# Output projection of a hybrid encoder layer: nine of twelve tile transposes as 32x32 blocks on DVE and quadrant copies on POOL

## The reference

```python
x = x + jnp.concatenate([a, p], axis=-1) @ w_out      # a: attention, p: pooling mixer
h2 = rmsnorm(x, norm2_g)
x = x + jnp.square(jax.nn.relu(h2 @ w_up)) @ w_down   # w_up: 1024 x 4096
```

## Time and profile before

| | |
|---|---|
| median of 3 runs | 1484.53 us (1484.3 to 1484.99) |
| the profiled execution | 1483.54 us, of which the trace spans 1481.8 us |
| PE busy in the span | 1471.5 us (99%) |
| DVE, ACT, POOL busy | 1042.6, 705.7, 401.1 us |
| granted TensorE clock | 1.00 |

### The profile page before, as it was taken

How to read it: one execution, slowest core, us unless ns; L and a number is a source line. 1 busy time by engine, 2 the same in 40 slices (tenths; PEclk the granted TensorE clock), 3 DMA queues, 4 the chain that set the end, 5 groups by cost and what they waited for, 6 DMA issues and landing times.

```text
span 1481.8 us, 23179 instructions
## 1 busy us (share of the span) xinstructions
PE 1471.5 (99%) x7884; PEld 1312.3 (89%) x7884; DVE 1042.6 (70%) x1301; ACT 705.7 (48%) x1195; POOL 401.1 (27%) x347
## 2 busy tenths in 40 slices
PE   9999999999999999999999999999999999999999
PEld 8999878888888889999999999999888888888887
DVE  6766799999856675544454545448888878878875
ACT  6223399999833344545454545456322322323220
POOL 3467599888910010000000000001320311311300
PEclk9999999999999999999999999999999999999999
DMA  8654331000246639343334323347744343343434
GB/s 262 154 121 112 98 90 24 20 11 14 83 146 250 219 113 413 132 146 125 129 113 157 134 109 134 137 155 291 264 157 153 104 149 122 125 156 105 137 99 183
DMA packets 89066, 209.10 MB, mean 141 GB/s; under 512 B 8240, under 2 KB 27568, under 8 KB 88880
## 3 DMA queue, kind: packets, MB, share of 16 engines
q1 hardware_dynamic: 86816, 197.27, 39.9%
q10 hardware_dynamic: 2192, 11.08, 1.8%
HBM read 129.93 MB, written 71.57 MB: 136 GB/s over the span
## 4 chain that ended last, share of the span: by engine, by line
PE 93%; DVE 2%; ACT 2%; POOL 1%; issue 1%; DMA 0%; ACTq 0%; POOLq 0%; DVEq 0%
PE ps L871 24%; PE ps L873 24%; PE ps L872 24%; PE ps L1134 6%; PE ps L1016 4%; PE ps L1144 3%; PE ps L1031 2%; PE ps L998 2%; PE ps L1032 2%; PE ps L1000 2%; ACT prob L1351 1%; PE ps L1154 1%; POOL prob L2414 0%; DVE pTlo L1744 0%; DVE nmax L1806 0%
## 5 line engine op out<-in xcount | busy, mean ns | idle before, releaser
L871 PE MATMUL ps<-h,wuhi 128*128 128x384 f32 (+1 forms) x904 | 301.5, 334 | 0.2 <-issue 0.2
L873 PE MATMUL ps<-h,wulo 128*128 128x384 f32 (+1 forms) x904 | 301.2, 333 | 0.0
L872 PE MATMUL ps<-h,wuhi 128*128 128x384 f32 (+1 forms) x904 | 301.2, 333 | 0.0
L871 PE MATMUL ps<-wdhi,hidhi 128*128 128x512 f32 x672 | 261.6, 389 | 0.0
L873 PE MATMUL ps<-wdhi,hidlo 128*128 128x512 f32 x672 | 261.6, 389 | 0.0
L872 PE MATMUL ps<-wdlo,hidhi 128*128 128x512 f32 x672 | 261.5, 389 | 0.0
L2220 DVE TENSOR_TENSOR yacc<-yacc,ps 128x1024 f32<-128x1024 f32 x167 | 203.2, 1217 | 78.1 <-PE ps L873 78.1
L1270 ACT ACTIVATE hidhi<-hin 128x1024 fp32r<-128x1024 f32 (+1 forms) x72 | 86.8, 1205 | 300.7 <-PE ps L873 292.8
L2134 DVE TENSOR_TENSOR u<-u,ps 128x384 f32<-128x384 f32 x96 | 53.1, 553 | 181.7 <-PE ps L873 181.7
L871 PEld LDWEIGHTS ps<-h,wuhi 128*128 128x128 f32 x904 | 169.7, 188 | 0.7 <-issue 0.4
L872 PEld LDWEIGHTS ps<-h,wuhi 128*128 128x128 f32 x904 | 169.8, 188 | 0.0
(11 more groups left out here) (217 smaller groups left out, 2804.2 us busy)
## 6 DMA issues: line engine op xcount, KB each, us to landing
hd<-hout SPq DMA_DIRECT2D x64, 384.0 KB, 3.2
hin<-hd SPq DMA_DIRECT2D x48, 512.0 KB, 3.7
hd<-hout SPq DMA_DIRECT2D x32, 576.0 KB, 2.8
hin<-hd SPq DMA_DIRECT2D x24, 768.0 KB, 4.4
wuraw<-in_w_up SPq DMA_DIRECT2D x17, 1024.0 KB, 6.0
wdraw<-in_w_down SPq DMA_DIRECT2D x8, 2048.0 KB, 9.4
h<-h2d ACTq DMA_DIRECT2D x7, 1536.0 KB, 11.6
x2in<-in_x SPq DMA_DIRECT2D x12, 512.0 KB, 3.3
```

The source lines that it names most:

```text
L871: pe.matmul(out, w_hi, m_hi, start=start, stop=False, skip_group_check=resumed)
L872: pe.matmul(out, w_hi, m_lo, start=False, stop=False, skip_group_check=resumed)
L873: return pe.matmul(out, w_lo, m_hi, start=False, stop=stop, skip_group_check=resumed)
```

## The change

For the first nine positions (`TURNED = TT - 3`) the tile is no longer transposed on PE. DVE writes the scaled tile into PSUM banks 4 and 5 (`junk_banks`, where ACT now also writes its unused squares), and then turns it in one instruction of 128x1024 elements (`turn_x2`), which transposes each 32x32 block in place in its group of 32 partitions (a quadrant), into the SBUF tile `x2turn`. POOL then puts the 16 blocks of 32 partitions by 256 elements where they belong, four for each quadrant of source and destination (`place_x2`), in four rounds of four, with a wait after each round. It writes them to one of three tiles `x2T`, so that ACT and DVE read the transposed tile from SBUF and not from PSUM. The blocks lie in another order inside the tile (`blocked`). The lists change as well: DVE's is now `residual(p)`, `split_c(p + 2)`, `scale_x2(p)`, `turn_x2(p)`, `lo_h2(p - 1)`; ACT's is `square_x2(p)`, `split_c(p + 2)`, `hi_h2(p - 1)`; SP stores the split tiles after the x tile's load. Some semaphores are merged.

```diff
+        TURNED = TT - 3
+        PLACES = (0, 1, 2, 0, 1, 2, 0, 1, 0)
...
         def h2_bank(q, b):

-            bank = b - 2 if b > 1 and q == TT // 2 - 1 else 4 + b
-            return ps[:, bank].rearrange("p (k c) -> p k c", k=4)
+            if 2 * q + b // 2 < TURNED:
+                return x2T[PLACES[2 * q + b // 2]][:].rearrange("p b k t -> p k b t")[:, b % 2 * 4:b % 2 * 4 + 4]
+            return blocked(h2_psum(q, b))
...
-                if p:
+                if p > TURNED:
                     transpose_x2(p - 1)
...
             for p in range(1, TT):
-                if p + 1 < TT:
-                    split_c(p + 1)
-                if p < TT - 2:
+                if p <= TURNED:
+                    residual(p)
+                    if p + 2 < TT:
+                        split_c(p + 2)
+                    scale_x2(p)
+                    if p < TURNED:
+                        turn_x2(p)
                     lo_h2(p - 1)
-                    residual(p)
-                    scale_x2(p)
...
+            def turn_x2(p):
+
+                dve.wait_ge(xs2_done, p + 1)
+                dve.wait_ge(x2_placed, 16 * p)
+                dve.transpose(x2turn[:], junk_banks().rearrange("p (k q c) -> p q k c", k=KT, q=4)).then_inc(x2T_done, 1)
...
+            def place_x2(p):
+
+                last = max((i for i in range(p) if PLACES[i] == PLACES[p]), default=None)
+                pool.wait_ge(x2T_done, p + 1)
+                if last is not None:
+                    if last % 2:
+                        pool.wait_ge(h2_lo, SLOTS * (last // 2 + 1))
+                    else:
+                        pool.wait_ge(h2_sum, 4 * (last // 2 + 1))
+                for r in range(4):
+                    for b in range(4):
+                        q = (b + r) % 4
+                        pool.tensor_copy(x2T[PLACES[p]][q * 32:q * 32 + 32, b], x2turn[b * 32:b * 32 + 32, q]
+                                         ).then_inc(x2_placed, 1)
+                    pool.wait_ge(x2_placed, 16 * p + 4 * r + 4)
+
             for p in range(TT - 1):
                 norm_x2(p)
-            norm_halves(1, TT, ms2_done, ss2_done)
+                if p < TURNED:
+                    place_x2(p)
```

More of the change, by code:

```diff
@@ L486, in wu_place, with blocked, h2_psum, h2_bank @@
             return (wuhi6, wulo6) if isinstance(w, int) and (w, o) == (0, 6) else (wuhi[o], wulo[o])
-        def h2_bank(q, b):
+        TURNED = TT - 3
+        PLACES = (0, 1, 2, 0, 1, 2, 0, 1, 0)
+        def blocked(tile):
+            return tile.rearrange("p k (b t) -> p k b t", b=4)
+        def h2_psum(q, b):
             bank = b - 2 if b > 1 and q == TT // 2 - 1 else 4 + b
             return ps[:, bank].rearrange("p (k c) -> p k c", k=4)
+        def h2_bank(q, b):
+            if 2 * q + b // 2 < TURNED:
+                return x2T[PLACES[2 * q + b // 2]][:].rearrange("p b k t -> p k b t")[:, b % 2 * 4:b % 2 * 4 + 4]
+            return blocked(h2_psum(q, b))
+        def turned_x2(p):
+            return (x2_placed, 16 * p + 16) if p < TURNED else (xT2_done, p - TURNED + 1)
+        def junk_banks():
+            return psw[:, 2048:3072]
         def h2_staged(q, a):
@@ L1160, in transpose_last @@
                 for k in range(4):
-                    mm = pe.transpose(h2_bank(TT // 2 - 1, 2)[:, k], xs2[:, k * P:(k + 1) * P], ident[:])
+                    mm = pe.transpose(h2_psum(TT // 2 - 1, 2)[:, k], xs2[:, k * P:(k + 1) * P], ident[:])
                 mm.then_inc(xT2_half, 1)
@@ L1692, in _ @@
             square_x2(0)
+            split_c(2)
             for p in range(1, TT):
-                if p + 1 < TT:
-                    split_c(p + 1)
+                if p <= TURNED:
+                    square_x2(p)
+                    if p + 2 < TT:
+                        split_c(p + 2)
+                    hi_h2(p - 1)
+                elif p + 1 < TT:
                     hi_h2(p - 1)
@@ L1706, in _ @@
                     square_last()
-                else:
+                elif p > TURNED:
                     square_x2(p)
@@ L2364, in window_step @@
                     ins = pool.tensor_tensor(part, part, edge[:, g, e * PAD:(e + 1) * PAD], ALU.mult)
[L2365 to L2368, removed]
+                ins.then_inc(win_part, 1)
+                pool.wait_ge(win_part, 2 * (s * GROUPS + g) + 1)
+                pool.tensor_scalar(sums, sums, 1.0 / w, 1.0, ALU.mult, ALU.mult).then_inc(win_part, 1)
+                pool.wait_ge(win_part, 2 * (s * GROUPS + g) + 2)
                 c0 = pool_pos(s)
@@ L2549, in norm_x2 @@
                 rsqrt_mean(rsx[:], msx[:], ssx[:], epsx[:], ms2_done, rs2_done, p)
+            def place_x2(p):
[4 more added lines that the diff above has]
+                        pool.wait_ge(h2_lo, SLOTS * (last // 2 + 1))
+                    else:
+                        pool.wait_ge(h2_sum, 4 * (last // 2 + 1))
[5 more added lines that the diff above has]
+                    pool.wait_ge(x2_placed, 16 * p + 4 * r + 4)
             for p in range(TT - 1):
                 norm_x2(p)
-            norm_halves(1, TT, ms2_done, ss2_done)
+                if p < TURNED:
+                    place_x2(p)
+            pool.wait_ge(ss_half, 1)
+            pool.tensor_tensor(msx[:], ssx[:], epsx[:], ALU.add).then_inc(ms2_done, 1)
+            pool.wait_ge(ms2_done, TT)
+            pool.wait_ge(ss2_done, TT)
+            pool.tensor_tensor(msx_b[:], msx[:], ssx_b[:], ALU.add).then_inc(ms2_done, 1)
+            pool.wait_ge(ms2_done, TT + 1)
             pool.wait_ge(xs2_done, TT - 1)
```

80 lines of the change are left out of this document (38 added, 42 removed).

## The result

The changed kernel takes 1500.28 us (median of 4 runs, 1499.19 to 1500.93) against 1484.54: ratio 1.0105, 95% interval 1.0087 to 1.0122, so 15.7 us slower. The profiled execution took 1499.19 us with a span of 1497.4, 15.6 more than before. The forecast was 1496.5, within 1480 to 1509.

A forecast was written before the change was run, and what follows sets the result against it. PE was taken to set the pace before; after the change a DVE-POOL loop of 26.7 us a pair against PE's 21.8 makes PE 10.7 us late at tile 9, plus 1.3: +12 us, 1496.5 us, range 1480 to 1509.

The forecast's parts named there:

- PE's work removed, 7.8 us: Output projection on PE: nine times eight transposes, 0.87 us each time, no longer run, 7.8 us in all.
- the bound of before: Output projection: PE sets the pace, busy for all of a tile's 11.78 us.
- Block transpose, 1.25 us: DVE's new 128x1024 block transpose from PSUM, one for each of nine tiles, takes 1.25 us.
- the rival with 2.14: DVE's block transpose costs 2.14 us, +6 to +7, 1503 us; chance 0.18 together with dear copies.
- Copies at 0.33 us, a tile 5.7: POOL's 16 copies of 32x256: 0.33 us each (0.25 to 0.40), 5.7 us a tile with the rounds' waits (4.4 to 6.8).
- The exclusion, on which the sign hung: DVE instructions with two SBUF inputs and POOL's SBUF reads exclude each other for nearly their whole length; 26.7 us a pair.
- PE late at tile 9's transposes: Tile 9 scaled at 546.1 us, PE's transposes there at 535.4 before, so PE is 10.7 us late.
- The last 1.3 us: Work behind tile 9's transposes fits in PE's 16.3 us only just, so 1.3 us is added.
- No exclusion for short copies: Rival: POOL's short copies slip in beside DVE's instructions, -7.8 + 3.3 = -4.5, 1480 us; chance 0.18.
- Side by side: Rival: POOL's four copies of a round overlap, 3 us a tile, -3 to 0, 1483 us; chance 0.22.
- Copies at 0.40 and DVE delayed at each: Rival: dearer POOL copies that also make DVE wait, +24, 1508.5 us; chance 0.18 together with the dear transpose.
- Reordered `split_c` at nothing: New place of `split_c`: delays the first scaling 2.6 us, hidden under PE's products of the next tile, so costs nothing.

The follow-up runs named there:

- the last experiment: Changed kernel with only tiles 0, 2, 4, 6 and 8 turned by DVE and placed by POOL, plus both reorders: 1481.12 us, ratio 0.9979 to the kernel before.
- the long memsets: Changed kernel with POOL's 16 copies a tile replaced by memsets 344 elements long, lasting as long as a copy: 1486.33 us, ratio 1.0013 to the kernel before.
- the short memsets: Changed kernel with POOL's 16 copies a tile replaced by memsets of the same 32x256 pieces: 1480.86 us, ratio 0.9978 to the kernel before.
- the run with one wait: Changed kernel with POOL waiting once a tile instead of after each round of four copies: 1500.7 us, ratio 1.011 to the kernel before.
- ACT's reorder: Changed kernel with ACT rounding the operand of tile p + 2 before it squares tile p: 1500.51 us, ratio 1.011 to the kernel before.
- one copy: Changed kernel with POOL making one 128x1024 copy a tile instead of 16 copies between quadrants: 1483.99 us, ratio 0.9998 to the kernel before.
- the transfers by way of DRAM: Changed kernel with SP placing the blocks by one transfer to DRAM and four back, instead of POOL's copies: 1495.47 us, ratio 1.0078 to the kernel before.
- three reorders: Changed kernel with POOL's factor made between rounds of copies (1499.42 us), with ACT rounding before squaring (1500.51 us), and with both (1498.64 us).

## Why the prediction was right, and where it was off

- **PE's work removed, 7.8 us, and the bound of before.** Right: the stage's account above closes with it, and the last experiment gets 4.4 us of it back for five tiles, less one wait of 1.1.
- **Block transpose, 1.25 us.** Right (1.249), though the fixed 0.18 us in its working stands in no row; the rival with 2.14 is out.
- **Copies at 0.33 us, a tile 5.7.** Too low, and outside my 4.4 to 6.8. By themselves they take 0.39 to 0.40, the dear end of my bounds and what the one-input rows gave for 256 elements; the memset that I took as the other end is another operation and cheaper (0.30). They also start 0.455 us apart, and that gap I had left out, while the 0.1 us for each round's wait is nothing. A tile costs 7.2 us.
- **The exclusion, on which the sign hung.** Right, and shown by the memsets against the copies: some 12 to 14 us. With the long memsets, which have none, the time is only 2 us above that of before. It runs both ways, but I priced it too high: in a long turn DVE loses 0.08 to 0.2 us at each instruction of `lo_h2`, 1.1 us in all, and 0.44 in a wait for the factor, and not 1.7 + 0.7; in a short turn POOL's copies last 8.7 us for 7.2, 1.5 more and not 1.3 + 1.3. DVE's wait for ACT, which I put at 2.47 us, was 2.26. "For nearly their whole length" holds for the long instructions of the earlier trace rows and not for these short ones. So the short turns were 12.3 us (11.3 forecast), the long ones 14.7 (15.4), the pair 27.0 (26.7): the copies were too cheap and the exclusion too dear, and that the two nearly cancel is luck.
- **PE late at tile 9's transposes.** 549.5 against 535.4 is 14.1 us, where I had 10.7: the first two turns took 11.5 and 12.2 and not 10.9 and 11.3 (1.5 us), three pairs 81.1 and not 80.1 (1.0), and the last stretch 14.95 and not 14.1 (0.9). That is the term that was too small, and nearly all of the 3.8 us between 1496.5 and 1500.28.
- **The last 1.3 us.** The size was right (1.5) and the reason wrong, which is luck: not the work behind tile 9, where PE has no wait before the MLP, but the clock, which I had left unbounded. Eight transposes and 16 products behind the wait of 11.9 us took 0.9 + 0.6 us longer. The clock's 2.7 us behind the 4.6 us wait didn't add to the delay, since PE then waited that much less for tile 9, whose turn DVE and POOL set.
- **No exclusion for short copies: out.** Its price, 1480 us, was that of the short memsets (1480.9), which have no exclusion, with a wait of 2.9 us for tile 9 where I had 3.3, and 1.7 us of slow work behind it, which I had not priced. But copies are longer than I took them; with their length and no exclusion the time is nearer that of the long memsets, 1486. **Side by side: out**, by the run with one wait. **Copies at 0.40 and DVE delayed at each**, 1508.5: the first half was true, the second less than priced (1.1 + 0.4 us in the long turns, nothing of weight in the short ones).
- **Reordered `split_c` at nothing.** Right as long as POOL's copies hold the turns: with ACT's reorder, which hands DVE the operand 1.2 us earlier, the time doesn't move (1500.5). It isn't free by itself. The new order puts a wait of 2.26 us for ACT behind each residual, and where no copies are in the way DVE's list is 23.0 us a pair against PE's 21.8 (one copy); with the transfers by way of DRAM ACT's reorder gained 2.8 us.

Of the 5.5 us between memsets of 0.38 and 0.30 us the two traces, whose spans differ by 3.1, show 4.4 at the start of the MLP: 3.9 us more of waiting for tile 9 (6.8 for 2.9), 0.3 for a second short wait, and 0.2 for slower work behind the wait (0.9 + 0.9 against 0.1 + 1.6). Still open: which property of a wait brings the lower clock. Its length alone doesn't: in the run with ACT's reorder 16 products behind a wait of 2.3 us took 5.53 us, at 0.69, and behind one of 3.2 us 3.92, at 1.00.

## What to carry to other kernels

When work moves to an idle engine, look for what the two engines share before counting its idle time: here DVE with two SBUF inputs and POOL reading SBUF, which held each other up until a pair of tiles took 27 us against PE's 21.8. The three reorders tried took at most 0.8 us off that, while less of the shared work took off all of it: half the tiles moved won 3 us, all nine lost 16. Price an unseen instruction from rows of the same operation first, by the distance from start to start and not by its duration, and a chain of transfers with what stands in front of it in its queue.

## What the runs showed of the hardware

- POOL and DVE alternate one instruction at a time where both are short: beside DVE's sums, stretched to 0.77 us, each copy took about 0.75 us, and each engine started one every 0.80 us. Neither starved, and one of each took less than the 1.06 to 1.18 us of the two by themselves.
- A POOL memset isn't held up by DVE's instructions with two SBUF inputs (301 to 310 ns for all 144), a POOL copy is (388 to 846 ns). Beside DVE's sums with one input in PSUM copies stay at 0.39 to 0.40 us.
- POOL's copies of 32 partitions x 256 elements take 0.39 us, in their own quadrant or across, and don't overlap though their quadrants are disjoint; 128x1024 in one copy took 1.04 us, against 7.2 us for the same elements in 16 copies, which start 0.455 us apart.
- DVE's block transpose of 128x1024 float32 took 1.25 us with runs of 32 elements from PSUM, against 2.14 with a stride of eight elements in SBUF.
- PE's granted clock was lower behind the waits of 4.6 us (0.56, 16 products in 6.50 us for 3.79) and 11.9 us (0.50) of the changed kernel. Behind one of 2.9 us in the run with memsets eight transposes ran at 1.00 and the 16 products after them at 0.67 (5.50 us for 3.89). Behind waits of 1.1, 2.4 and once 3.2 us it stayed at 1.00.
